# First-layer opening reordered, gate sums and decay rows placed earlier, and a tenth buffer for expert weights

## What is computed

```python
for i in range(2):
    # modulation: six vectors per stream from a matrix of 1024 x 6144
    sh1, sc1, g1, sh2, sc2, g2 = split(silu(c) @ ada_w[i] + ada_b[i], 6)
    hl = modulate(rms_norm(xl, norm_mix[i]), sh1, sc1)
    if i == 0:   # hc: the same for 256 context tokens with c_ctx
        yl = even_mixer(hl, hc, ...)      # gated DeltaNet, two directions, 4 heads, + pooling
    else:
        yl = short_conv_mixer(hl, ...)
    xl = xl + g1 * yl
    xl = xl + g2 * expert_choice_ffn(modulate(rms_norm(xl, norm_ffn[i]), sh2, sc2), ...)
```

## Time and profile before

| | us |
|---|---|
| median of three runs | 1412.75 |
| the profiled execution, its own time | 1415.97 |
| span in its trace (first to last instruction) | 1414.2 |
| PE busy, share of the span | 1190.0, 84% |
| DVE busy | 623.5, 44% |
| ACT busy | 432.1, 31% |
| POOL busy | 78.0, 6% |
| DMA: moved, mean rate | 338.65 MB, 239 GB/s |
| granted TensorE clock, mean share of full speed | 0.929 |

### The profile page before, as it was taken

The page is one execution under the profiler, slowest core; times in us unless marked ns, Lnnn a source line. Parts: engine busy times, 40 slices in busy tenths (PEclk is TensorE's granted clock), DMA queues, the critical chain, the costliest instruction groups (busy, mean ns, idle before and its releaser), DMA issues.

```text
span 1414.2 us, 19546 instructions
## 1 busy us (share of the span) xinstructions
PE 1190.0 (84%) x8265; PEld 884.5 (63%) x8265; DVE 623.5 (44%) x1136; ACT 432.1 (31%) x777; POOL 78.0 (6%) x118
## 2 busy tenths in 40 slices
PE   5899889998986656679998665767999999999887
PEld 2777558785852113159985221315999778899766
DVE  3655784556430001146743000113994455545574
ACT  2536334322310000034231000002544563443462
POOL 3000123440000000000000000000000000100000
PEclk7999899999989889899999888988999979999898
DMA  9944854326589999995458999999344304355000
GB/s 327 328 140 167 298 182 176 120 86 224 227 336 410 409 409 408 410 363 179 179 230 351 410 409 409 409 409 346 120 160 140 119 18 148 134 179 179 1 1 30
DMA packets 125099, 338.65 MB, mean 239 GB/s; under 512 B 8657, under 2 KB 11590, under 8 KB 125014
## 3 DMA queue, kind: packets, MB, share of 16 engines
q1 hardware_dynamic: 117536, 334.51, 62.4%
q10 hardware_dynamic: 7478, 2.91, 0.8%
HBM read 336.35 MB, written 1.05 MB: 239 GB/s over the span
## 4 chain that ended last, share of the span: by engine, by line
PE 59%; DMA 25%; DVE 10%; ACT 3%; issue 1%; ACTq 1%; SPq 0%; DVEq 0%
PE bank L685 9%; PE bank L687 9%; PE bank L686 9%; DMA expert_slots<-in_w_up_dram 6%; DMA weight_ring<-in_w_down_dram 5%; DMA arena<-in_w_gate_dram 4%; DMA weight_ring<-in_w_up_dram 3%; DVE arena L1880 3%; PE bank L975 3%; PE bank L592 2%; PE bank L1141 2%; DMA expert_slots<-in_w_gate_dram 2%; DMA arena<-in_w_up_dram 2%; PE bank L550 2%; DMA arena<-in_w_down_dram 2%; PE bank L812 2%
## 5 line engine op out<-in xcount | busy, mean ns | idle before, releaser
L685 PE MATMUL bank<-input_high,weights_high 128*128 128x256 f32 (+1 forms) x992 | 290.6, 293 | 8.2 <-DVE input_low L1880 7.5
L687 PE MATMUL bank<-input_high,weights_low 128*128 128x256 f32 (+1 forms) x992 | 284.1, 286 | 0.0
L686 PE MATMUL bank<-input_low,weights_high 128*128 128x256 f32 (+1 forms) x992 | 283.8, 286 | 0.0
L1880 DVE TENSOR_TENSOR weights_low<-weight_ring,weights_high 128x1024 fp32r<-128x1024 f32 x144 | 176.1, 1224 | 174.6 <-ACT weights_high L1436 174.2
L685 PEld LDWEIGHTS bank<-input_high,weights_high 128*128 128x128 f32 x992 | 188.5, 190 | 13.5 <-issue 10.6
L1436 ACT ACTIVATE weights_high<-weight_ring 128x1024 fp32r<-128x1024 f32 x144 | 151.7, 1055 | 143.8 <-PE bank L687 143.4
L687 PEld LDWEIGHTS bank<-input_high,weights_low 128*128 128x128 f32 x992 | 188.6, 190 | 0.0
L686 PEld LDWEIGHTS bank<-input_low,weights_high 128*128 128x128 f32 x992 | 188.1, 190 | 0.7
L1880 DVE TENSOR_TENSOR arena<-arena,bank 128x512 f32<-128x512 f32 (+1 forms) x38 | 24.8, 652 | 272.9 <-PE bank L975 244.2
L975 PE MATMUL bank<-weight_ring,arena 128*32 128x512 f32 x480 | 68.4, 705 | 44.6 <-DMA weight_ring<-in_w_up_dram 24.3
L975 PEld LDWEIGHTS bank<-weight_ring,arena 128*32 128x32 f32 x480 | 15.9, 121 | 93.8 <-issue 41.1
(11 more groups left out here) (410 smaller groups left out, 1742.7 us busy)
## 6 DMA issues: line engine op xcount, KB each, us to landing
weight_ring<-in_ada_w_dram SPq DMA_DIRECT2D x24, 2048.0 KB, 9.0
weight_ring<-in_w_gate_dram SPq DMA_DIRECT2D x20, 2048.0 KB, 21.3
weight_ring<-in_w_down_dram SPq DMA_DIRECT2D x16, 2048.0 KB, 23.7
arena<-in_w_up_dram SPq DMA_DIRECT2D x12, 2048.0 KB, 24.2
arena<-in_w_down_dram SPq DMA_DIRECT2D x12, 2048.0 KB, 23.8
expert_slots<-in_w_up_dram SPq DMA_DIRECT2D x10, 2048.0 KB, 24.1
weight_ring<-in_w_up_dram SPq DMA_DIRECT2D x10, 2048.0 KB, 23.8
weight_ring<-in_even_w_in_dram SPq DMA_DIRECT2D x9, 2048.0 KB, 8.9
```

The lines of the kernel that those rows point to most:

```text
L685: pe.matmul(b[:, 0:width], hi[:, k, :], XHI[:, k, t0:t0 + width], start=k == 0, stop=False)
L686: pe.matmul(b[:, 0:width], hi[:, k, :], XLO[:, k, t0:t0 + width], start=False, stop=False)
L687: mm = pe.matmul(b[:, 0:width], lo[:, k, :], XHI[:, k, t0:t0 + width], start=False, stop=k == KD - 1)
L1880: return dve.tensor_tensor(out_, a, b, op)
```

## The change

1. **Opening.** PE does only `ada` chunk 0 before the token transposes, and chunks 1 to 3 after them. The first two of the four output tiles of the first product are plain float32 products of the ring's weights with `hT`. `warm(10)` becomes `warm(4)`. The transposes of `meta` and the late vectors move behind the first product. The chunk with columns 512 of `ev_w_in` is loaded before `ada` chunk 4. ACT issues the vector loads in three parts (6 before the squares, 4 between them, 7 after), and only the first three entries of `small_src`. ACT, not DVE, scales the context stream, twice: once into the high part, once in place.
2. **Middle.** The `gc` products stand behind the second tile of the pooling product; the transposes of the decay rows stand right behind that product, ahead of the q sums. DVE does what follows `gc` between groups 1 and 2, the low part of the rows ahead of the copies of v; the sums of pooling group 3 become a step `poolsum` behind the first `rows`. POOL fills `ROW_OF` after all eight L2 scalings (`l2_done`), not after `gam_args`.
3. **Experts.** `MOE_SLOTS` is 10; the new slot lies at word 4096 of the arena and waits as slot 8 does. Other tiles of the stage move; `Y` and `RT` have one buffer in place of two, so `combine` runs for each group, and its residual additions run four times per layer in place of three. The other four small loads (`ssd_dt_bias`, `ssd_a_log`, twice `ssd_d`) and the second layer's router are issued by ACT in the first expert stage, behind the softmax exponential.

```diff
-MOE_SLOTS = 9
+MOE_SLOTS = 10
...
-    steps = ada + [("turnrows", 0, 0, 0), ("rows", 0, 0, 0)]
+    steps = ada + [("rows", 0, 0, 0), ("poolsum", 0, 3, 0)]
...
-        expert_slots = arena_slots + [split_slots[:, i, :] for i in range(SPLIT_SLOTS)] + [at(0, CHUNK)]
+        expert_slots = arena_slots + [split_slots[:, i, :] for i in range(SPLIT_SLOTS)] + [at(0, CHUNK), at(CHUNK, CHUNK)]
...
-        n_small = len(small_src)
+        n_small = 3
...
-        for src, adas in (((ev, 0), 1), ((ev, 512), 1), ((ev, 1024), 1), ((ev, QKV), 0), ((ev, QKV + 512 + 16), 3)):
...
+        for src in ((ev, 0), (ev, 512), None, (ev, 1024), None, None, (ev, QKV), (ev, QKV + 512 + 16), None, None, None):
...
             ada_mm()
-            ada_mm()
-            pe.wait_ge(scalar_drained, ada["copied"] - 1)
-            ada_turn()
             for tt in range(2 * TT):
...
+                if i == 0:
+                    arrive(cn)
+                    for m in range(2):
+                        b = opener()
+                        for k in range(KD):
+                            if m == 0:
+                                pe.wait_ge(h_scaled, k + 1)
+                            mm = pe.matmul(b[:, 0:T], chunk(cn)[:, k, m * P:m * P + P], hT[:, k, 0:T], start=k == 0, stop=k == KD - 1)
+                        closer(mm, (names, mt + m))
+                for m in range(0 if i else 2, 4):
...
-            warm(10)
+            warm(4)
             first_product(0, 0, T, s_open, s_close, "qkv")
+            late_vectors()
...
-                    if g == 2:
-                        combine((0, 1), "partial")
-                    elif g == 3:
-                        combine((2,), "partial")
+                    if g:
+                        combine(g - 1, "partial")
...
-                if slot_of(cn) == LATE_SLOT:
+                if slot_of(cn) >= LATE_SLOT:
                     sp.wait_ge(scalar_filled, mark[("h2", stream[cn][1])])
...
-            pool.wait_ge(gam_args, 1)
+            pool.wait_ge(l2_done, 8)
...
+            for half in range(2):
+                ks = range(4 * half, 4 * half + 4)
+                for k in ks:
+                    act.activation(XHI1[:, k, T:2 * T], hT[:, k, T:2 * T], ACT.Identity, scale=gain[:, k, 1:2],
+                                   bias=MOD[:, 0, k, 1:2]).then_inc(context_high, 1)
...
+                else:
+                    for dst, src in small_src[n_small:]:
+                        act.dma_start(dst, src, allow_slow_non_contiguous=True).then_inc(ssd_small_in, 16)
+                if ly == 0:
+                    act.dma_start(RT, router[1].rearrange("(k p) e -> p k e", p=P)).then_inc(router_in, 16)
...
-                    if g >= 2:
+                    if g:
                         for m in range(KD):
                             residual(ly, 40, m)
```

More of the change, by code:

```diff
@@ L626, in _ @@
                     (s_close if tt % 2 else v_close)(mm, ("tokens", tt))
-            for i in range(2):
+            for i in range(3):
                 ada_mm()
@@ L743, in _ @@
                     ada_step()
-                elif kind == "turnrows":
-                    pe.wait_ge(masks_ready, 4)
-                    pe.wait_ge(gam_rows, 1)
-                    b = v_open()
-                    for u in range(UNITS):
-                        mm = pe.transpose(b[0:SELROWS, u * P:u * P + P], GC2[:, u, :], ident[:, :])
-                    v_close(mm, "gamma_rows")
                 elif kind == "rows":
@@ L1452, in _, with load_vecs @@
             act.activation(ce, VT[:, 0, 0:16], ACT.Exp, scale=-1.0).then_inc(c_exp, 1)
+            later_vecs = [name for name in vec_src if name not in first_vecs]
+            def load_vecs(names):
+                for name in names:
+                    g, r, k = vec_at[name]
+                    act.dma_start(VEC[r:r + k, g, :], vec_src[name]).then_inc(vec_in, 16)
+            load_vecs(later_vecs[:6])
             def rstd(src, nr):
@@ L1559, in _ @@
                 drained(act.activation(CB[:, t % 4, 0:w, 1:1 + T], bank(b, w, T), ACT.Copy))
-                high()
+                if t >= 3:
+                    high()
+                if t == 3:
+                    b = take()
+                    drained(act.activation(XH[:, :, 0:META], bank(b, KD, META), ACT.Copy))
+                    act.wait_ge(small_in, 16 * n_small)
+                    act.activation(alog, alog, ACT.Exp)
                 if t % 4 == 3:
@@ L1592, in _ @@
                     ins.then_inc(gam_exps, 1)
+                    ada_copy()
+                    act.wait_ge(vector_filled, mark["gamma_rows"])
+                    act.wait_ge(l2_done, 4)
+                    b = VB[(mark["gamma_rows"] - 1) % 4]
+                    act.activation(ROWS[0:SELROWS, :], b[0:SELROWS, :], ACT.Copy).then_inc(rows_high, 1)
                 b = take()
@@ L1601, in _ @@
                     ada_copy()
-                elif kind == "turnrows":
-                    act.wait_ge(vector_filled, mark["gamma_rows"])
-                    b = VB[(mark["gamma_rows"] - 1) % 4]
-                    act.activation(ROWS[0:SELROWS, :], b[0:SELROWS, :], ACT.Copy).then_inc(rows_high, 1)
                 elif kind == "rows":
@@ L1633, in _ @@
                     act.wait_ge(scaled, 2 * HEADS)
-                    for ly in range(2):
-                        act.dma_start(RT[:, ly], router[ly].rearrange("(k p) e -> p k e", p=P)).then_inc(router_in, 16)
+                    act.dma_start(RT, router[0].rearrange("(k p) e -> p k e", p=P)).then_inc(router_in, 16)
                 elif kind == "w" and (d, a) == (1, 3):
@@ L1673, in experts @@
                     b = take()
-                    drained(act.activation(Y[:, g % 2, 0:512], b[:, :], ACT.Copy))
+                    drained(act.activation(Y[:, 0:512], b[:, :], ACT.Copy))
                 logs()
@@ L2002, in _ @@
                     drained(dve.tensor_copy(hT[:, 4 * kh:4 * kh + 4, t_ * P:t_ * P + P], bank(b, 4, P)))
-            for i in range(3):
+            for i in range(4):
                 ada_bias()
@@ L2055, in _ @@
                     ada_bias()
-            split()
-            split()
+            for _ in range(4):
+                split()
             b = take()
@@ L2080, in l2_scale, with pool_sums @@
                     stt(QT[:, i - 4, :], QT[:, i - 4, :], float(P) ** -0.5, l2_buf(i), MUL, MUL).then_inc(l2_done, 1)
-            for g in range(4):
-                if g:
-                    ada_bias()
-                split()
-                b = take()
+            def pool_sums(g):
                 group = PADP[:, 4 * g:4 * g + 4, :]
-                drained(dve.tensor_copy(group[:, :, 8:72], bank(b, 4, 64)), True)
                 sums, width = group, 80
@@ L2129, in _ @@
                     ada_steps += 1
-                elif kind == "turnrows":
-                    b = take()
-                    dve.wait_ge(rows_high, 1)
-                    low = ROWS[32:SELROWS, :]
-                    drained(tt(low, b[32:SELROWS, :], low.bitcast(F32), SUB))
+                elif kind == "poolsum":
+                    dve.wait_ge(vector_drained, n["v"])
+                    pool_sums(h)
                 elif kind == "kk":
```

220 lines of the change are left out of this document (115 added, 105 removed).

## The result

The changed kernel took 1395.71 us (median of four runs, 1389.82 to 1399.5); four runs of the kernel before had 1413.61 as their median. The ratio is 0.9861, 95% interval 0.9836 to 0.9886: 1.4% less, 18 us by the medians and 20 by the ratio. The profiled execution took 1396.42 us, its span is 1394.5 in place of 1414.2, so 19.7 us went. The forecast was 1391 in a range of 1383 to 1404.

A forecast was written before the change was run, and what follows sets the result against it. Weight DMA was taken to bound the expert stages, PE or DVE the stretches before. Terms -9.5, -7.5, -4.9 and -0.3 sum to -22.2: 1415.97 to 1393.8, less 3.2 gives 1391 us, range 1383 to 1404.

The forecast's parts named there:

- rival (a): Opening gives half, its first tiles running at the low clock: gain 4 us, total 1396; chance 0.20.
- The opening: Start through first projections: earlier weight chunk and plain tiles start product 1 at 54.9 for 64.40, -9.5 us.
- the moved transposes now cost 0.95: Opening, after product 0: transposes of meta and vectors, hidden or beside the splits before, now add 0.95 us.
- The middle: Stretch around the first rows product, bounded by DVE: reordering frees DVE and shortens PE's wait, -7.5 us, bounds -3 and -9.
- I change nothing: Middle: POOL's later ROW_OF fill frees 2 us of DVE at the scalings but meets poolsum instead, so no adjustment.
- Layer 0: First expert stage: tenth slot's 5.1 us gain given back to moved small loads, -0.3 us, bounds -5.1 and +3.
- The price of the packets: All 1024 4-byte ssd_d packets cost 5.5 us of DMA time, won in the opening, paid in the first expert stage.
- Rival (e): 4-byte packets cost next to nothing beside 4 KB ones; layer 0 gives 4.8 us more, total 1386; chance 0.07.
- Layer 1: Second expert stage: tenth slot fills the DMA hole from 759.5 to 763.5 and its edges, -4.9 us.
- (c): Gains before the experts not carried, PE waiting for modulation loads in the mixer; total 1406; chance 0.09.
- (d): 4-byte packets in the expert stage cost over 0.55 us each, making it slower; total 1421; chance 0.03.
- the signs of being wrong: Projection chunk after 42, plain tiles at clock 0.5, PE waiting for gamma_rows, or last down product under 12 us earlier.

The follow-up runs named there:

- best: Changed kernel with late small loads in the first layer's mixer, 8 dummies before modulation chunk 3's product, one dummy for four before the first product: 1395.12 us, ratio 0.9834.
- before_mixer: Kernel before the change with only the four late small loads moved from opening to mixer: product 1 at 64.49 us, 0.2 later; no whole time given.
- split_first: Changed kernel with all four tiles of the first product split again, no plain tiles: 1406.54 us, ratio 0.9919.
- small_opening: Changed kernel with the four late small loads back in the opening: product 1 at 62.45 us, 3.6 later; last down product of layer 0 at 598.72, 1.8 earlier.
- slots9: Changed kernel with nine expert weight slots instead of ten: layer 1 stage 227.4 us against 222.4, layer 0 stage 264.3 against 263.7; no whole time given.
- small_mixer: Changed kernel with the four late small loads issued in the first layer's mixer instead of the first expert stage: 1391.28 us, ratio 0.9834.

## Why the prediction was right or wrong

The time lay in the range, 5 us above the forecast, at the 1396 of rival (a). Half of the 5 us isn't in any term. The profiled execution before lay 3.2 us above its median, and I took these off; the one after lies 0.7 above its own. Between the two profiled executions 19.6 us went, where the sum has 22.2. Step by step:

- **The opening** was the term that missed: -5.5 for -9.5. Three things came in. The modulation chunk 3 landed at 35.08, where I had kept the 34.1 of before. Its product ran at 1.2 GHz after a wait of 4.17 us, 3.56 us for 1.92. And "the moved transposes now cost 0.95" left out that they wait for ACT's copy of the first results, 0.86 us. These are 3.5 of the 4 us; best got the second back with eight dummies, and one in place of four ahead of the plain tiles. Rival (a) named the number but not the place: it had the low clock in the plain tiles, and these ran at full clock (7.07 us for two, where I had 6.9).
- What the same term had right, it had for a partly wrong reason: I derived it from the chunk's landing at 39.5 in place of 44.5. It landed at 40.50, 5.4 us behind chunk 3 as reckoned, but before_mixer shows that in the old order nothing hung on it; PE waited for the splits. It was the plain tiles that took the splits out of the way (split_first), and only then was the chunk the next thing (small_opening).
- **The middle** held: -8.3 for -7.5, in a stretch where the same code took 276.6 to 279.2 us. The composition was different. "I change nothing" for POOL was wrong: 2.6 us of DVE were won at the scalings, and the 2.5 lost at `poolsum` are hidden, as PE is full there (5.00 of 5 us from 151.9). The low clock behind the wait is gone too: at the first product of the chain of small products the gain since product 1 is 9.7 us. 1.4 of it were given back by the output projection, which is within the spread. The Trainium skill (SBUF — State Buffer, section "SBUF: two separate sides") was right on the stall and also says where it does not come: an instruction of VectorE that isn't in a 2-port mode loses only with two SBUF inputs, against a GpSimd operation that reads SBUF. Here the copies out of PSUM kept their 2.48 us, and a product of two SBUF inputs went from 0.43 to 2.94. By that rule I had 4.4 for the middle; the trace gave 8.3, as the place it stalls is covered.
- **Layer 0** came within 1.2 us, +0.9 for -0.3, and that is in part luck. The slot was put at 5.1 us and gives 2.5 with the packets away; the packets were put at 5.5 and cost 5.2. Each of the two was reckoned as if the other weren't there, and where there is a hole the packets cost 3.2. What made up for the small slot is a term that the sum had at nothing: with nine slots and no packets in the stage the changed order takes 261.0 us, where the kernel before took 262.8. So other changes of the stage won some 1.8 us; which ones is open.
- The price of the packets, put at 5.5 us, was 5.2 and 5.5 in two runs of their own, 4.7 in the mean of all, and 4.6 in the opening. Rival (e) falls with it. The floor that the Trainium skill gives (DMA: Bandwidth & Descriptors, section "Bandwidth", some 10.5 ns a packet, for transfers that GpSimd issues) lies between the 9 and 12 ns that the records book for a packet here, and misses what 4-byte packets cost the weights.
- **Layer 1** held: -5.1 for -4.9, and slots9 shows 4.9 of it as the slot's. Rivals (c) and (d) didn't happen: what was won before the experts was carried to them.
- -1.9 us behind layer 1 were not forecast. They come before the gates of the second block, 132.7 us for 134.6, and begin in the last combine, whose first 16 small products took 1.93 us where they took 2.78. It is the clock of these two executions, and not the change: variants of the changed kernel took up to 137.5 us there.
- Of the signs, three of being right stayed away with the opening's 4 us: the plain products started at 42.34 (for 39.5), product 1 at 58.82 (for 55), and the first `rows` came 12.8 us earlier (for 16 to 17). None of the signs of being wrong came, the last one by 0.9 us.

## What to carry to other kernels

Ask of each early landing what PE waited for before it: here a chunk 4 us earlier was worth nothing until two tiles could use it without the splits. Put loads of single 4-byte elements where the DMA has nothing to do, never into a stage that lives on its rate (a hole of 4 us took only 2 of their 5), and price them by what the others lose. When an operation is moved out of a neighbour's way, look for who stands beside it next, and whether that one has cover.

## What the runs showed of the hardware

- 4-byte packets that alternate with 4 KB packets take 0.073 to 0.081 us of an engine each out of the weights' rate, with 0.009 booked; 64-byte packets of the same queue are booked with 12 ns and cost nearly nothing more (388 GB/s for the core beside 858 of them in 10 us).
- A wait of about 4 us ahead of chunk 3's product was followed by 1.2 GHz in every run that had it (3.25 to 3.64 us in place of 1.92, eight runs), and a wait of 2.52 us in split_first too (3.64 us); waits of up to 2.68 us ahead of chunk 2's product were followed by 1.92 us in all those eight. With dummies in the wait chunk 3's product ran at 2.4 GHz in all three. In four runs the low level went on through the dummies (3.31 us in place of 2.00 in small_mixer), and product 1 came 1.0 to 1.2 us later still (59.79 to 60.05 for 58.82), with the plain tiles at full clock. In small_opening the plain tiles themselves ran low behind a wait of 2.33 us (8.86 us for 7.07).
- A VectorE product on two SBUF operands stands still while GpSimd selects in SBUF (0.43 to 2.94 us); beside GpSimd's memset the sums took the same 1.97 us as without it, and the copies out of PSUM took 2.48 us beside the select as without it.
